# Two block sums made by accumulating DMA, and the residual's two parts sent as one 512-column operand

## What is computed

```python
def swiglu(h, w_gate, w_up, w_down):
    return (jax.nn.silu(h @ w_gate) * (h @ w_up)) @ w_down
...
for i in range(DEPTH):
    h = h + 0.5 * swiglu(rms_norm(h, norms[i, 0]), ...)
    ...  # attention and S5, or sparse and differential attention
    h = h + 0.5 * swiglu(rms_norm(h, norms[i, 2]), ...)
    gate = jax.nn.sigmoid(rms_norm(h, norms[i, 3]) @ ple_w_gate[i])
    h = h + gate * (p[i] @ ple_w_proj[i])
```

## Time and profile before

| | us |
|---|---|
| median of 3 runs (1890.55 to 1890.62) | 1890.58 |
| the profiled execution | 1890.69 |
| its span | 1888.9 |
| TensorE busy | 1860.7 (99%) |
| DVE busy | 1357.9 (72%) |
| ACT busy | 890.9 (47%) |
| POOL busy | 261.4 (14%) |
| DMA, all queues | 179.88 MB, mean 95 GB/s |

### The profile page before, as it was taken

The page is one execution under the profiler, slowest core; times in us unless marked ns, Lnnn a source line. Parts: engine busy times, 40 slices in busy tenths (PEclk is TensorE's granted clock), DMA queues, the critical chain, the costliest instruction groups (busy, mean ns, idle before and its releaser), DMA issues.

```text
span 1888.9 us, 31440 instructions
## 1 busy us (share of the span) xinstructions
PE 1860.7 (99%) x11418; PEld 1617.9 (86%) x11418; DVE 1357.9 (72%) x1981; ACT 890.9 (47%) x1503; POOL 261.4 (14%) x204
## 2 busy tenths in 40 slices
PE   8999999999999999999999999999989999999998
PEld 6899988777799998887899998877657899998886
DVE  8788788774988874357888864279984988874355
ACT  7355542245555554224455553134573655554222
POOL 0000001212200000225000001073243100000225
PEclk9999999999999999999999999999999999999999
DMA  5232333333233333323333343332101333333321
GB/s 179 90 109 94 109 98 108 93 100 89 75 99 100 111 105 118 103 76 99 102 89 101 111 123 90 99 109 67 57 1 46 91 100 100 111 103 119 102 77 56
DMA packets 56753, 179.88 MB, mean 95 GB/s; under 512 B 12144, under 2 KB 12144, under 8 KB 56656
## 3 DMA queue, kind: packets, MB, share of 16 engines
q1 hardware_dynamic: 54656, 173.69, 29.9%
q0 software_dynamic: 928, 3.02, 0.5%
q10 hardware_dynamic: 1088, 2.10, 0.3%
HBM read 175.04 MB, written 3.15 MB: 94 GB/s over the span
## 4 chain that ended last, share of the span: by engine, by line
PE 88%; DVE 7%; ACT 2%; POOL 1%; issue 1%; DMA 0%; DVEq 0%; SPq 0%; POOLq 0%; ACTq 0%
PE ps L2288 36%; PE ps L2250 26%; PE ps L2232 18%; PE ps L2736 2%; PE ps L2399 1%; DVE sm L1265 1%; PE ps L2635 1%; DVE work L1241 1%; DVE w_lo L384 1%; POOL sumsq L1541 1%; DVE stat L1239 1%; DVE x_lo L436 1%; ACT prob L1970 0%; PE ps L2654 0%; PE ps L2450 0%
## 5 line engine op out<-in xcount | busy, mean ns | idle before, releaser
L384 DVE TENSOR_TENSOR w_lo<-raw,w_hi 128x1024 fp32r<-128x1024 f32 x174 | 231.9, 1341 | 217.1 <-ACT w_hi L376 215.8
L376 ACT ACTIVATE w_hi<-raw 128x1024 fp32r<-128x1024 f32 x186 | 194.1, 1054 | 300.0 <-PE ps L2250 248.7
L2288 PE MATMUL ps<-xs_hi,w_hi 128*128 128x256 f32 x1088 | 308.4, 283 | 0.5
L2288 PE MATMUL ps<-xs_lo,w_hi 128*128 128x256 f32 x1088 | 308.1, 283 | 0.0
L2288 PE MATMUL ps<-xs_hi,w_lo 128*128 128x256 f32 x1088 | 308.0, 283 | 0.0
L2250 PE MATMUL ps<-act_hi,w_hi 128*128 (+1 forms) x720 | 280.6, 390 | 0.0
L2250 PE MATMUL ps<-act_lo,w_hi 128*128 (+1 forms) x720 | 280.3, 389 | 0.0
L2250 PE MATMUL ps<-act_hi,w_lo 128*128 (+1 forms) x720 | 280.2, 389 | 0.0
L2232 PE MATMUL ps<-x_hi,w_hi 128*128 128x512 f32 x640 | 258.1, 403 | 8.9 <-ACT w_hi L376 7.6
L2232 PE MATMUL ps<-x_hi,w_lo 128*128 128x512 f32 x640 | 250.7, 392 | 0.0
L2232 PE MATMUL ps<-x_lo,w_hi 128*128 128x512 f32 x640 | 250.6, 392 | 0.0
(11 more groups left out here) (406 smaller groups left out, 3547.5 us busy)
## 6 DMA issues: line engine op xcount, KB each, us to landing
raw<-in_weights SPq DMA_DIRECT2D x322, 512.0 KB, 3.6
h<-in_xT ACTq DMA_DIRECT2D x4, 512.0 KB, 6.8
out<-result SPq DMA_DIRECT2D x4, 512.0 KB, 3.0
p_raw<-in_pT POOLq DMA_DIRECT2D x2, 512.0 KB, 4.0
scratch_u<-u_sc SPq DMA_DIRECT2D x1, 512.0 KB, 5.9
u_grp<-scratch_u SPq DMA_DIRECT2D x1, 512.0 KB, 4.3
scratch_y<-y_grp SPq DMA_DIRECT2D x2, 256.0 KB, 3.0
y_ch<-scratch_y SPq DMA_DIRECT2D x1, 512.0 KB, 3.5
```

The costliest lines, as they stand in the source:

```text
L376: act.activation(w_hi[:, slot], raw[:, slot], ACT.Copy).then_inc(hi_ready, 1)
L384: dve.tensor_tensor(w_lo[:, slot], raw[:, slot], w_hi[:, slot].bitcast(F32), SUB)\
L2288: last = pe.matmul(ps[:, bank, 0:HALF], w[:, at, cols], x[:, k], start=(start and k == 0 and part == 0), stop=(stop and k == KH - 1 and pa ...
```

## The change

- **Operand.** `x_hi` and `x_lo` become the two parts of one tensor `x_parts`, and a new function `paired` does B21 and T4: four matmuls of 512 columns with the high weights (high part of x into columns 0 to 255 of the bank, low part into 256 to 511), then four of 256 with the low weights. Both halves of the bank have to be added afterwards: `gate_left` gets a second addition, and the right gate a copy by ACT and an addition by DVE (`gate_right`) ahead of its silu.
- **Sums.** T1 and T3 (the first two sums) are made by DMA: POOL's new `block_sums` loads two blocks from the weights in HBM, waits for them, and issues two DMAs that add a third block to both. Even tiles use `w_sum[:, 0:2]`, odd ones a new buffer `other_sums` over the first rows of `x_lo`. The first odd one waits for the last plain chunk. DVE keeps the other two sums.
- **Order.** T4 alternates between slots and T2 doesn't, so their high and low parts are made one by one (`fourth_hi`, `second_hi`, `fourth_lo`, `second_lo`), except in the first tiles. The product of a tile moves from its own end to after the sums in the next tile, and `gate_right` takes its place.

The diff, cut to its core:

```diff
-        x_hi, at_x = sb("x_hi", [P, KD, T], F32R)
-        x_lo, at_x_lo = sb("x_lo", [P, KD, T], F32R)
+        x_parts, at_x = sb("x_parts", [P, 2, KD, T], F32R)
+        x_hi, x_lo = x_parts[:, 0], x_parts[:, 1]
+        at_x_lo = at_x + 4 * KD * T
...
+        other_sums = over("other_sums", [P, 2, T], at_x_lo)
...
+        def loaded_sums(b):
+            return other_sums[:] if b % 2 else w_sum[:, 0:2]
...
                 for k in range(2):
                     dve.wait_ge(raw_loaded[slot + k], turn_of(first, 2 * b + k, i) * 16 + 16)
-                dve.tensor_tensor(w_sum[:, 0:2], own[:, 0:4:3],
-                                  own[:, 2].unsqueeze(1).to_broadcast([P, 2, T]), ADD)\
-                   .then_inc(fast["w_sums"], 1)
-                dve.wait_ge(fast["w_sums"], counted(3, f, i, b, 1))
-                dve.tensor_tensor(w_sum[:, 2], w_sum[:, 0], own[:, 3], ADD)\
+                dve.wait_ge(fast["blocks_added"], 32 * counted(1, f, i, b, 1))
+                dve.tensor_tensor(w_sum[:, 2], loaded_sums(b)[:, 0], own[:, 3], ADD)\
                    .then_inc(fast["w_sums"], 1)
...
             def gate_left(i, b):
                 dve.wait_ge(fast["product"], counted(5, f, i, b, 4))
                 dve.wait_ge(fast["copied"], counted(4, f, i, b, 1))
-                dve.tensor_tensor(t1[:, b % 2, 0:HALF], ps[:, banks_of(b)[1], 0:HALF],
-                                  part_sum[:, 0, HALF:], ADD).then_inc(s["gate_scaled"], 1)
+                left = ps[:, banks_of(b)[1]]
+                dve.tensor_tensor(t1[:, b % 2, 0:HALF], left[:, 0:HALF],
+                                  part_sum[:, 0, HALF:], ADD).then_inc(fast["folded"], 1)
+                dve.wait_ge(fast["folded"], counted(1, f, i, b, 1))
+                dve.tensor_tensor(t1[:, b % 2, 0:HALF], left[:, HALF:], t1[:, b % 2, 0:HALF],
+                                  ADD).then_inc(s["gate_scaled"], 1)
+
+            def gate_right(i, b):
+                dve.wait_ge(fast["half_copied"], counted(1, f, i, b, 1))
+                dve.tensor_tensor(t1[:, b % 2, HALF:], ps[:, banks_of(b)[0], 0:HALF],
+                                  t1[:, b % 2, HALF:], ADD).then_inc(fast["right_scaled"], 1)
...
             def opening_tile():
 
                 weight_sums(pair, 1)
                 gate_left(pair, 0)
                 own_lo(pair, 1, 0)
                 sums_lo(pair, 1, 1)
                 up_right(pair, 0)
                 sums_lo(pair, 1, 0)
                 own_lo(pair, 1, 1)
                 up_left(pair, 0)
-                product(pair, 0)
+                gate_right(pair, 0)
 
             def fast_tile(i, b):
 
+                dve.wait_ge(fast["t_ready"], counted(2, f, i, b, 2))
                 weight_sums(i, b + 1)
-                sums_lo(i, b + 1, 0)
+                product(i, b - 1)
+                fourth_lo(i, b + 1)
+                second_lo(i, b + 1)
                 gate_left(i, b)
                 own_lo(i, b + 1, 0)
                 up_right(i, b)
                 sums_lo(i, b + 1, 1)
                 own_lo(i, b + 1, 1)
                 up_left(i, b)
-                product(i, b)
+                gate_right(i, b)
...
+        def block_sums(pool, f, first):
+            plain = PLAINS[f]
+            pair = plain // 2
+            def sums(i, b, opening=False):
+                dst = loaded_sums(b)
+                if opening:
+                    if b:
+                        pool.wait_ge(chunk_used, first + 2 * plain)
+                else:
+                    pool.wait_ge(fast["t_ready"], counted(2, f, i, b - 2, 2))
+                    pool.wait_ge(fast["w_sums"], counted(2, f, i, b - 2, 1))
+                gate, up = (A["weights"][bass.ds(i * 4 + (first + 2 * b + k), 1)]
+                            .rearrange("a p b f -> (a p) (b f)") for k in range(2))
+                pool.dma_start(dst[:, 0], gate[:, 0:T]).then_inc(fast["blocks_loaded"], 16)
+                pool.dma_start(dst[:, 1], up[:, T:]).then_inc(fast["blocks_loaded"], 16)
+                pool.wait_ge(fast["blocks_loaded"], 32 * counted(1, f, i, b, 1))
+                pool.dma_start(dst[:, 0], up[:, 0:T], accum_op=ADD).then_inc(fast["blocks_added"], 16)
+                pool.dma_start(dst[:, 1], up[:, 0:T], accum_op=ADD).then_inc(fast["blocks_added"], 16)
+            sums(pair, 0, opening=True)
+            sums(pair, 1, opening=True)
+            with pool.Fori(pair + 1, NF // 2, 1) as i:
+                sums(i, 0)
+                sums(i, 1)
...
             def silu_right(i, b):
                 act.wait_ge(chunk_used, i * 4 + (first + 2 * b + 2))
                 act.wait_ge(s["prod_done"], i * 2 + (b - 1) + NF * f)
-                act.activation(t1[:, b % 2, HALF:], ps[:, banks_of(b)[0], 0:HALF], ACT.Silu)\
+                act.activation(t1[:, b % 2, HALF:], ps[:, banks_of(b)[0], HALF:], ACT.Copy)\
+                   .then_inc(fast["half_copied"], 1)
+                act.wait_ge(fast["right_scaled"], counted(1, f, i, b, 1))
+                act.activation(t1[:, b % 2, HALF:], t1[:, b % 2, HALF:], ACT.Silu)\
                    .then_inc(s["silu_done"], 1)
...
+            def paired(bank, at, both, start, stop, done):
+                for k in range(KH):
+                    pe.matmul(ps[:, bank], wf_hi[:, at, k * P:(k + 1) * P], both[:, :, k],
+                              start=(start and k == 0), stop=False, skip_group_check=True)
+                for k in range(KH):
+                    last = pe.matmul(ps[:, bank, 0:HALF], wf_lo[:, at, k * P:(k + 1) * P],
+                                     both[:, 0, k], start=False, stop=(stop and k == KH - 1),
+                                     skip_group_check=True)
+                last.then_inc(done, 1)
...
-                product(left_bank, at["B21"], *unmixed(5), True, True, fast["product"])
+                paired(left_bank, at["B21"], both(5), True, True, fast["product"])
...
-                product(first_bank, at["T4"], *unmixed(6), False, True, chunk_used)
+                paired(first_bank, at["T4"], both(6), False, True, chunk_used)
```

More of the change, by code:

```diff
@@ L327, in encoder @@
         fast = {n: sem(f"fast_{n}") for n in (
+            "blocks_loaded", "blocks_added",
             "x_gained", "x_normed", "x_sums", "x_hi", "x_ready", "w_sums", "t_hi",
-            "t_ready", "product", "copied")}
+            "t_ready", "product", "copied", "folded", "half_copied", "right_scaled")}
         tab = sem("tab")
@@ L389, in counted, with sums_counted @@
             return i * (2 * each) + (each * (b - PLAINS[f] + FAST_BEFORE[f]) + n)
+        def sums_counted(f, i, b, n):
+            done = 3 * FAST_BEFORE[f] - 2 * f
+            if isinstance(i, int) and 2 * i + b < PLAINS[f] + 2:
+                return done + 2 * (2 * i + b - PLAINS[f]) + n
+            return i * 6 + (done + 3 * (b - PLAINS[f]) - 2 + n)
         def halves_of(first, b):
@@ L502, in sums_lo, with fourth_lo, second_lo @@
                 at = halves_of(first, b)[("T24", "T13")[which]]
-                src = w_sum[:, 2:4] if which == 0 else w_sum[:, 0:2]
+                src = w_sum[:, 2:4] if which == 0 else loaded_sums(b)
                 turned = isinstance(i, int) and 2 * i + b < plain + 2
-                dve.wait_ge(fast["t_hi"], counted(2, f, i, b, 2 - which if turned else 1 + which))
+                dve.wait_ge(fast["t_hi"], sums_counted(f, i, b, 2 - which if turned else 3))
                 dve.tensor_tensor(wf_lo[:, at], src, wf_hi[:, at].bitcast(F32), SUB)\
+                   .then_inc(fast["t_ready"], 1)
+            def fourth_lo(i, b):
+                at = halves_of(first, b)["T4"]
+                dve.wait_ge(fast["t_hi"], sums_counted(f, i, b, 1))
+                dve.tensor_tensor(wf_lo[:, at], w_sum[:, 3], wf_hi[:, at].bitcast(F32), SUB)
+            def second_lo(i, b):
+                at = halves_of(first, b)["T2"]
+                dve.wait_ge(fast["t_hi"], sums_counted(f, i, b, 2))
+                dve.tensor_tensor(wf_lo[:, at], w_sum[:, 2], wf_hi[:, at].bitcast(F32), SUB)\
                    .then_inc(fast["t_ready"], 1)
@@ L1628, in _ @@
                 .then_inc(const_ready, 1)
+            pool.wait_ge(rstd_ready, 1)
+            block_sums(pool, 0, STARTS[0])
             s5_loads(pool)
@@ L1634, in _ @@
             sum_squares(pool, 2)
+            pool.wait_ge(rstd_ready, 3)
+            block_sums(pool, 1, STARTS[3])
             load_embedding(pool, 0, 3)
@@ L1637, in _ @@
             sum_squares(pool, 4)
+            pool.wait_ge(rstd_ready, 5)
+            block_sums(pool, 2, STARTS[5])
             sum_squares(pool, 5)
@@ L1640, in _ @@
             sum_squares(pool, 6)
+            pool.wait_ge(rstd_ready, 7)
+            block_sums(pool, 3, STARTS[8])
             load_embedding(pool, 1, 8)
@@ L1721, in sums_hi, with fourth_hi, second_hi @@
                     act.wait_ge(fast["product"], counted(5, f, i, b - 1, (3, 5)[which]))
```

(20 more changed lines are left out.)

3 lines of the change are left out of this document (2 added, 1 removed).

## The result

The changed kernel takes 2009.5 us (median of four runs, 2004.9 to 2015.4) against 1890.6: 1.063 times the time before, 95% interval 1.0615 to 1.0647. The prediction was 1893.3, at most 1907. Its profiled execution has a span of 2010.1 us, 121.2 longer than before.

A forecast was written before the change was run, and what follows sets the result against it. It took TensorE, busy 99% of the span, as the bound: -6.9 us from the pair plus 9.6 from four opening stalls gave +2.7, a forecast of 1893.3 us, range 1886 to 1907 for eight in ten.

The forecast's parts named there:

- what the pair gives: TensorE, B21 and T4: eight fewer matmuls and weight loads a tile, 0.10 us, over 68 tiles 6.9 us off.
- The prediction's other estimate: TensorE: by the skill page's 2.5 ns fixed cost a matmul, the change takes off only 1.4 us.
- The opening stall: Second tile's sums wait for the last plain chunk; TensorE stalls L - 6.7 = 2.4 us, four stretches, 9.6 us added.
- L: Latency from the sum buffer's release, in ACT's sight, to both sums being in place: 9.1 us, bounds 7.5 and 14.6.
- The steady loop: Steady tiles: L is hidden up to 13 us; beyond that, half a microsecond a tile for each over.
- The change on POOL and the DMA engines: Step on the 272 added DMAs on POOL's queue: loading pair 4.3, adding pair 4.0, extra 0.8, L = 9.1 us.
- 0.8, about a quarter, a choice: Adding pair of transfers: 0.8 us extra for reading the destination, on top of 4.0 us.
- The upper bound of 14.6: Highest latency from release to sums: every transfer at 4.3 us and the adding pair at twice that.
- a share of 0.66 to 0.83: DMA engines in the fast stretches: share rises from 0.33 to 0.66, or 0.83 if adds cost double; below one.
- rival C: Much slower: L over 13 also throttles the steady tiles; at 14.6, +73 us, 1963 us; chance 0.06.
- Within that tile the next things are just in time: Tile after the opening stall: T13 low 1.2 us after the start where 1.4 is allowed, T24 low 2.6 against 2.9.
- DVE's 1.22 us: Steady tile: DVE loses line 491 (1.22 us), 0.24 us less net after additions; costed at nothing because hidden.

The follow-up runs named there:

- the pair alone: The changed kernel without the transfers: DVE makes the first two sums itself and POOL's four calls are gone; 1891.3 us, 1.0004.
- four buffers, two early: The changed kernel with four sum buffers in the place of two, the two used first free early; 1890.4 us, 1.0000.
- the plain second pair: The changed kernel with the second pair of transfers as plain copies, both accumulations left out, output not the reference's; 1911.4 us, 1.0115.
- the pair alone with the order mended: The changed kernel without the transfers, DVE's right gate in the opening and ACT's first partial copy in the last tile moved forward; 1886.4 us, 0.9978.
- four buffers, two early, with the order mended: The changed kernel with four sum buffers, two free early, and the opening's right gate and last tile's first partial copy moved forward; 1886.1 us, 0.9977.

## Why the prediction was wrong

**Right: what the pair gives.** The steady tile is 9.99 us for 9.98, where nothing holds it. In the version with the pair alone that is 5.4 us in the 56 steady tiles and 0.4 in the first ones, about 6, as the row of line 2232 said. The prediction's other estimate, 1.4 us in all from the 2.5 ns a matmul of the Trainium skill (TensorE: Matmul & The Clock Gate, "Wait — 56ns, not 53.3ns?"), is too small for these matmuls.

**Right: both mechanisms and their formulas.** The opening stall was to be L - 6.7; with DVE's sums at 88.45, L counted from 77.29 is 11.2 and the stall 4.5; the first tile takes 14.76 us for 10.31 in the version with four buffers, two early, 4.45 over. The steady loop was to throttle from L = 13 by half a microsecond each; (7 + 16.3) / 2 = 11.65 against 11.63.

**Wrong: the step "The change on POOL and the DMA engines", L = 9.1 us.** It failed in two terms. The adding pair was 4.0 + 0.8; it took 7.0 in the opening and 8.2 in a steady tile. "0.8, about a quarter, a choice" was the weakest number of the sum: nothing in the rows spoke for a quarter, and the other end, twice a plain transfer or 8.6, was where it came out. And one L, worked out in the opening's terms, was used for both places. The loading pair was 4.3, right for the opening (4.2 with the wake-up) but 0.7 + 7.3 in the steady tiles, since by then the rings also carry SP's loads and the pair before; with no add in the kernel they still took 6.7 in the mean. The upper bound of 14.6 was even below the 16.3 measured: it took 4.3 for a transfer with 768 KB ahead, all plain. I had worked out a share of 0.66 to 0.83, written "below one" and gone on; for a latency the share in the microseconds of the transfer counts, and there it was 0.72 to 1.07.

**Wrong: rival C's chance, 0.06.** With the adding pair at twice a plain one and the loading pair at 4.3 the prediction's own terms give L = 13.6, over the margin of 13; with the wait for other transfers it was far over. Its price held: at 16.3 its own formula gives 60 x 1.65 = 99 us for the steady tiles, and steady and last tiles together lost 93.

**Missed: the second tile.** "Within that tile the next things are just in time" was not so. Where no transfer can be late, the pair's new order costs 1.25 us there with DVE making the sums (11.37 for 10.12), through the right gate that now needs a copy, an addition and a silu one after the other, the addition last in DVE's opening: with the addition moved forward the second tile falls to 10.44, and to 9.99 with the transfers. After a long stall the clock adds to it, see the last section.

**Right: DVE's 1.22 us are worth nothing in the steady tile.** They were put at nothing and stayed there: 9.99 us with DVE making the sums and without.

## What to carry to other kernels

A transfer that takes the place of a hidden vector operation has to close its own circle, release to reuse, within the number of buffers times the tile; write that circle down with the latency that the rings have at that moment, not their mean share, and count an accumulating byte as two to three plain ones (2.6 here). If the engine that is relieved was not the bound, the best outcome is no change. And when a change is made of two parts, look at each alone: here one part earned 6 us and lost as much at the edges of the stretches, which only showed once the other part was gone; moving two operations gave 5 of them back.

## What the runs showed of the hardware

**The accumulating transfer.** POOL's issue of the first takes 0.89 us and of the second 1.21, where a plain one takes 0.54 to 0.57; groups of 34, busy us, mean ns, idle time before and what ended it:

```profile
L1600 POOL DMA_DIRECT2D other_sums<-in_weights x34 | 41.1, 1209 | 0.5 <-issue 0.5
...
L1599 POOL DMA_DIRECT2D w_sum<-in_weights x34 | 30.2, 888 | 201.4 <-DMA w_sum<-in_weights 201.4
```

Its queue has 31392 packets for 74.34 MB, and 22688 for the same bytes when the second pair is plain:

```profile
q0 software_dynamic: 22688, 74.34, 11.3%
```

That is 8704 packets more for 136 accumulating transfers, 64 each; by the packets' sizes in the trace, 256 KB go in 128 packets of 2 KB in the place of 64 of 4 KB.

**The clock after a stall.** Windows of the changed kernel around the stall in the first opening; the third number from the end is the granted clock:

```profile
87.50:91.80 4.30, 0.08 (x1) 0.00 (x0) 3.28 (x6) 2.16 (x3) 1.54 (x2) 1.00 0.21 80
91.80:94.00 2.20, 2.15 (x11) 2.15 (x12) 2.20 (x3) 1.05 (x3) 0.23 (x1) 0.61 0.98 143
94.00:96.00 2.00, 2.00 (x13) 2.00 (x12) 1.67 (x4) 0.30 (x1) 0.81 (x2) 0.58 0.87 231
96.00:98.00 2.00, 1.94 (x17) 1.76 (x16) 0.00 (x0) 0.77 (x3) 0.31 (x1) 1.00 1.00 344
```

After 4.3 us without a matmul the grant falls from the 2.4 GHz level to the 1.2 GHz one for 3.4 us, 92.27 to 95.68: 15 matmuls in a row are 0.21 us apart in the place of 0.12, some 1.5 us lost, a third of the stall's own length on top of it. In the other three openings TensorE waits 4.6, 5.4 and 4.3 us, and the grant falls for 3.4, 6.8 and 3.4 us. In the version with the plain second pair it waits 2.1, 2.0, 2.4 and 2.3 us; the grant falls only after the third, for 3.4 us, and stays at 1.00 after the others. So with waits of a little over 2 us it goes either way, and with these four of over 4 it fell each time.

**The end of the program.** From the issue of the last transfer of the result to the end of the span it is 4.3 us in the kernel before and in both versions with the pair alone, and 5.8 in all nine kernels in which POOL issues 272 transfers. With 112 of the 272 on ACT's queue it is 5.1, and 4.4 where the two adds are one transfer and POOL issues 204. The rows of the issue, for the pair alone with the order mended (span 1885.6) and for four buffers, two early, with the order mended (span 1886.6):

```profile
1881.25 0.50 SPq L1555 DMA_DIRECT2D out<-result  x1
```

```profile
1880.75 0.59 SPq L1554 DMA_DIRECT2D out<-result  x1
```

What takes the 1.5 us is not shown.
